# Down rows in 8 KB runs, gate and up columns with a step of four: an expert layer on one Trainium2 core

## The reference

```python
top_v, top_i = lax.top_k(e_in_group, TOP_K)          # 2 of 32 experts per token
def one_block(args):
    tok, e, w = args
    xb = xt[tok]                                     # (block, 1024)
    hb = jax.nn.silu(xb @ w_gate[e]) * (xb @ w_up[e])  # w_gate, w_up: (1024, 512)
    return (hb @ w_down[e]) * w[:, None]             # w_down: (512, 1024)
```

## Time and profile before

| | |
|---|---|
| median of 3 runs | 1695.05 us (1694.65 to 1702.41) |
| profiled execution | 1699.27 us |
| its span, first to last instruction | 1697.4 us |
| mean granted TensorE clock | 0.859 |
| PE busy | 1240.7 us (73%) |
| bytes moved by DMA | 400.32 MB |
| of it gate, up and down loads | 82 loads of 1 MB each |

### The profile page before, as it was taken

The page is one execution under the profiler, slowest core; times in us unless marked ns, Lnnn a source line. Parts: engine busy times, 40 slices in busy tenths (PEclk is TensorE's granted clock), DMA queues, the critical chain, the costliest instruction groups (busy, mean ns, idle before and its releaser), DMA issues.

```text
span 1697.4 us, 25988 instructions
## 1 busy us (share of the span) xinstructions
PE 1240.7 (73%) x9514; PEld 604.3 (36%) x9515; DVE 443.3 (26%) x968; ACT 177.8 (10%) x464; POOL 214.4 (13%) x364
## 2 busy tenths in 40 slices
PE   7959997679855786776669999888545567877730
PEld 1124444343322443343212444665243233444310
DVE  0021116743620111111037000553461011111116
ACT  0000013410100000000001000442000000000000
POOL 0000000000011332222110000000001122333220
PEclk9979996879877998898779999679757689999875
DMA  9952321026279999999996541101008999699940
GB/s 345 358 181 99 111 66 46 1 75 207 104 297 415 378 415 415 383 416 416 414 368 238 137 134 47 65 1 50 0 38 354 416 416 416 241 416 387 386 145 37
DMA packets 103315, 400.32 MB, mean 236 GB/s; under 512 B 14724, under 2 KB 15012, under 8 KB 81768
## 3 DMA queue, kind: packets, MB, share of 16 engines
q1 hardware_dynamic: 79544, 341.88, 51.6%
q0 software_dynamic: 16848, 55.23, 9.6%
q10 hardware_dynamic: 6884, 2.71, 0.6%
HBM read 383.18 MB, written 16.74 MB: 236 GB/s over the span
## 4 chain that ended last, share of the span: by engine, by line
PE 45%; DMA 35%; DVE 9%; ACT 4%; issue 3%; DVEq 1%; SPq 1%; POOL 0%; ACTq 0%; POOLq 0%
DMA ring<-in_w_down_dram 25%; PE ps L702 20%; DMA ring<-in_w_up_dram 5%; PE ps L877 5%; PE ps L660 5%; PE ps L675 5%; PE ps L895 3%; PE ps L792 2%; ACT hT L578 2%; DMA mbias<-in_b_ada_dram 2%; PE ps L825 1%; DVE sums L1076 1%; DMA qkv<-ybuf 1%; DMA ring<-in_w_gate_dram 1%; PE ps L777 1%
## 5 line engine op out<-in xcount | busy, mean ns | idle before, releaser
L877 PE MATMUL ps<-ring,xs 128*32 128x256 f32 x4736 | 316.6, 422 | 132.5 <-DMA ring<-in_w_up_dram 90.5
L877 PEld LDWEIGHTS ps<-ring,xs 128*32 128x32 f32 x4736 | 177.7, 120 | 265.6 <-issue 193.9
L702 PE MATMUL ps<-ring,hT 128*128 128x512 f32 x576 | 250.3, 596 | 4.5 <-ACT hT L542 2.3
L895 PE MATMUL ps<-ring,hm 128*32 128x256 f32 x2368 | 156.2, 404 | 38.4 <-ACT hm L628 27.1
L702 PEld LDWEIGHTS ps<-ring,hT 128*128 128x128 f32 x576 | 109.8, 191 | 143.7 <-issue 136.9
L1309 DVE TENSOR_TENSOR hp<-sg,ps 128x128 f32<-128x128 f32 x74 | 21.3, 288 | 329.8 <-ACT sg L625 329.7
L895 PEld LDWEIGHTS ps<-ring,hm 128*32 128x32 f32 x2368 | 70.8, 114 | 99.3 <-ACT hm L628 41.7
L1317 DVE COPY yo<-ps 128x256 f32<-128x256 f32 x74 | 31.4, 425 | 246.1 <-DMA ybuf<-yo,idy 150.2
L675 PE MATMUL ps<-ring,cond 128*2 128x512 f32 x192 | 91.3, 631 | 5.7 <-issue 4.5
L660 PE MATMUL ps<-ring,cond 128*2 128x512 f32 x192 | 84.8, 605 | 10.1 <-ACT cond L520 10.1
L702 PE MATMUL ps<-ring,qT 128*128 128x512 f32 x192 | 84.8, 604 | 2.3 <-ACT qT L542 2.3
(11 more groups left out here) (198 smaller groups left out, 922.1 us busy)
## 6 DMA issues: line engine op xcount, KB each, us to landing
ring<-in_w_gate_dram SPq DMA_DIRECT2D x82, 1024.0 KB, 15.4
ring<-in_w_up_dram SPq DMA_DIRECT2D x82, 1024.0 KB, 15.6
ring<-in_w_down_dram SPq DMA_DIRECT2D x82, 1024.0 KB, 15.6
ring<-in_w_ada_dram SPq DMA_DIRECT2D x48, 1024.0 KB, 10.2
ring<-in_w_qkv_a_dram SPq DMA_DIRECT2D x12, 1024.0 KB, 4.9
ring<-in_w_qkv_b_dram SPq DMA_DIRECT2D x12, 1024.0 KB, 6.8
modb<-mdram POOLq DMA_DIRECT2D x16, 512.0 KB, 7.6
qkv<-ybuf POOLq DMA_DIRECT2D x2, 3072.0 KB, 19.4
```

Of the source, the lines that this page charges most:

```text
L702: ins = mm(ps[:, 2 * t + hf, :], lhs[:, k, t * P:(t + 1) * P], raw[:, slot, kk * D + hf * 512:kk * D + (hf + 1) * 512], start=(k == 0), st ...
L877: ins = mm(ps[j * BLK:(j + 1) * BLK, 1, 0:W].rearrange("p (a n) -> p a n", a=2), xs[:, k, :], w[:, :, at:at + FW], start=(k == 0), stop=(k ...
L895: ins = mm(ps[j * BLK:(j + 1) * BLK, 5, 0:WD], hm[:, 2 * c + q, :], ring[:, slot + GU + c, q * D + j * WD:q * D + (j + 1) * WD], start=(c ...
```

## The change

Two edits, which belong together. In the load of down, partition p now takes rows 4p to 4p+3 of the expert's 512: rows 4p and 4p+1 in slot 4, rows 4p+2 and 4p+3 in slot 5. In `gate_up`, group j now takes the columns j, j+4, j+8, ... of gate and of up instead of the 128 columns from 128j on, so the feature in column f of group j is 4f + j, which is the row that partition f now holds for step j.

```diff
                         else:
                             src = w_down[l, bass.ds(e, 1)]
-                            src = src.rearrange("a (c m p) n -> p (a c) m n", c=2, m=2)[:, s - GU, :, :]
+                            src = src.rearrange("a (p c m) n -> p (a c) m n", c=2, m=2)[:, s - GU, :, :]
                             dst = dst.rearrange("p a (m n) -> p (a m) n", m=2)
                         sp.dma_start(dst, src).then_inc(moe_land[l][s], 16)
...
                             for j in range(G):
-                                at = kk * DE + j * FW
                                 ins = mm(ps[j * BLK:(j + 1) * BLK, 1, 0:W].rearrange("p (a n) -> p a n", a=2), xs[:, k, :],
-                                         w[:, :, at:at + FW], start=(k == 0), stop=(k == KD - 1))
+                                         w[:, :, kk * DE + j:(kk + 1) * DE:G], start=(k == 0), stop=(k == KD - 1))
```

## The result

The changed kernel takes 1842.72 us (median of 4 runs) against 1697.38 us for the kernel before measured beside it: a ratio of **1.086**, interval 1.0822 to 1.0898. It is slower by about 145 us, where the forecast was 1690 and no slowdown.

What follows compares the result with a forecast made beforehand. Loads were taken to pace 33 experts and blocks the rest; -5.0 us for the down loads, 0 for the moving operand and 0 for gathers gave 1690 us against a median of 1695.05, with a range of 1684 to 1868.

Steps and rivals of the forecast that it cites:

- What bounds the kernel: Expert stages: loads pace 33 experts at about 15.5 us each; blocks pace 25 of 74 blocks, 6.81 us apart.
- The loads of down: Runs of 8 KB for 4 KB save 0.075 us a load, two loads in 33 load-paced experts: -5.0 us.
- The estimate after the Trainium skill: Down loads: about 3 cycles fixed cost a packet, 0.06 us saved an expert, making the sum -1.9 us instead of -5.0.
- The moving operand: L877 (gate_up) reading columns with a step of four: cost 0 as the likeliest, staying at 3.50 us.
- the doubled L877: Rival: the step doubles gate_up's time, 1865 us; chance 0.17 for about one and a half to two times.
- The price of a doubled `gate_up`: Expert blocks at 10.3 us instead of 6.81: 88 us in 25 blocks plus 82 us in 16 further, together +170.
- The term for the other 16 blocks: Further blocks of load-paced experts: two blocks take 20.6 us, 5.1 over the 15.5 us of loads; 82 us.
- The late gathers: Gathers land some 0.4 us later: cost 0; rival at most 12 us, 1703; chance 0.07, shared with a slower L877.
- Faster by a larger gain: Rival on the down loads: longer runs save the undiminished 0.15 us a load, -10 us, 1685 us; chance 0.12.

Runs made afterwards that it cites:

- the pair of kernels with step two: Kernel before, gate_up groups taking every second column of a half; down in 8 KB runs: ratio 0.9989; in 4 KB runs: ratio 1.0016.
- the run at 2 KB: Kernel before with down rows loaded in runs of 2 KB, each row in two halves: ratio 1.0080, +13.6 us.
- the probes: Kernel before with single matmuls added after the adaLN loop, operands at various steps and pitches: 405 ns a round contiguous, 423 step two, 846 step four.
- plain doubling: Kernel before with every gate_up matmul issued once more into an unused PSUM bank, all contiguous: 1828.54 us, ratio 1.0753.

## Why the prediction was wrong

**What bounds the kernel** was right: two regimes, 33 load-paced experts and 25 block-paced blocks, and the place where a longer `gate_up` would show.

**The loads of down** came out as forecast, as far as it is shown: 416 to 419 or 420 GB/s, and 4.6 us by the pair of kernels with step two, against -5.0 in the sum. No run with 8 KB runs is faster than the kernel before beyond its interval. The estimate after the Trainium skill ("DMA: Bandwidth & Descriptors", section "Why small descriptors are slow (HBM only)"), -1.9 us, is lower than the 4.6 but inside what was measured; the run at 2 KB, +13.6 us, speaks for the larger price. Two readings were a little off, without effect on the sum: from 2 to 4 KB the time per load falls by 5.5 to 6%, not 5, and `xs` is ready 1.9 us before the next L877, not 2.3, as its row starts at 601.34 and lasts 0.45.

**The moving operand** is the step that failed. The prediction took 0 for the step of four, from the weight loads of the transposes beside an ordinary weight load: it read 193 ns against 190 as "a stream with a step can deliver an element in about the time an fp32 matmul needs". Two things were wrong in that. The transposes' rows don't show the effect: they cost the same at step two and at step four, and an ordinary fp32 weight load goes from 192 to 330 ns. An ordinary fp32 load with a step would have told, and none of rows 12 to 14 is one. And the slack that fp32's slow pace seemed to leave isn't there: a line takes as long as two fp32 elements at fp32's own pace. In place of the 0 for this term, 3.50 us became 7.35 us, and with it 6.81 us a block became 10.66. The rival that came true is the doubled L877, at 2.1 instead of 2. Its reason was off as well, as far as it looked to the four streams: one stream alone is slowed as much.

The rule of the Trainium skill that was weighed there ("Advanced Engine Details and Errata", section "SBUF Cachelines": at least two hits on a 16-byte line) is what the probes show: step two 4% longer, pairs at a pitch of 4 or 8 elements 4 to 6%, step four twice. It was given less weight than a row that looked near and was not. The sentence of the Trainium skill's "SBUF — State Buffer" page (section "Door 1: The DMA port swizzle") by which four fp32 are a free step does not hold for TensorE's moving operand: 846 against 405 ns, and step three already costs half as much again (a factor of 1.56).

**The price of a doubled `gate_up`** was too high: +170 us, where plain doubling measured +128. With 3.85 us a block the same working gives 189, and the change cost 145. The 25 block-paced blocks are the firm part (96 us). The term for the other 16 blocks charged each with 5.1 us as if every expert stood alone. What it left out is that loads run ahead while blocks pace, so that the next short expert starts at once. The starts of `gate_up` in three blocks of the changed kernel show it:

```profile
674.53 7.44 PE L876 MATMUL ps<-ring,xs 128*32 128x256 f32 x64 [1.20 <-DMA ring<-in_w_up_dram]
685.97 7.43 PE L876 MATMUL ps<-ring,xs 128*32 128x256 f32 x64 [0.67 <-issue]
697.92 7.50 PE L876 MATMUL ps<-ring,xs 128*32 128x256 f32 x64 [1.18 <-issue]
```

The first two are experts of one block each (blocks of one expert start 10.66 us apart), 11.4 and 11.9 us long, though the loads of an expert take 15.5; the same two took 23.5 us together before and take 23.4 now. Counted over all starts of blocks in both traces, 53 of the steps from one block to the next hold +146 us. 25 x 3.85 = 96 us of it is the firm part, so the other 28 took 50 us where the working has 16 x 5.8 = 93. The last five steps of layer 0 are even 8 us shorter than before (59.4 instead of 67.5). That blocks at a low clock lose little by the step is a second thing that reduces the sum, but it isn't needed: plain doubling, which has no such relief, kept the same share of its price (128 of 170) as the step (145 of 189). What each takes by itself wasn't tried. The range held the time of 1842.7 only because its upper end, 1868, had been drawn to that rival with its price too high; the sign of the forecast was wrong.

**The late gathers** stay open: the waits for gathers vary between profiles (46 to 72 us in all) by more than the effect would be, and in the changed kernel the longer block covers them (21.8 us of waits in the whole run). **Faster by a larger gain** did not happen.

## What to carry to other kernels

Count the 16-byte lines of SBUF that a moving fp32 operand touches: by the two probes, a matmul takes 0.84 ns a record times its columns or times about twice its lines, whichever is more, so neighbours must stay in pairs, and a step of two (4%) is the last cheap one. Before taking "no cost" from a row of another operation, ask whether that row changes at all with the size that is in question; a probe of 16 matmuls answers it. Longer runs in HBM are worth something only where loads pace, here about 0.3% for 4 KB to 8 KB, so there is little that may be paid for them on another engine.

## What the runs showed of the hardware that was not expected

- A single fp32 stream with a step of four or more takes 1.7 to 1.76 ns a column and record against 0.84 contiguous, and two or four groups of 32 array columns side by side take about as long as one (13.1 and 13.8 us against 13.5 for 16 rounds).
- A matmul that is held by its lines doesn't follow the granted clock: 7.55 us at 0.74 and 7.46 at 1.00 for `gate_up`, where contiguous it goes from 6.51 at 0.55 to 3.66 at 1.00.
- The stationary operand of an ordinary fp32 matmul follows the rule too (for 128 columns 192 ns, 196 at step two, 330 at step four); a transpose's weight load does not show it (209 ns at step two, 212 at step four).
